# A hybrid decoder block: the first half of the second MLP matrix in quads of seven products too, all low halves on VectorE, a new order of parts

## The reference

```
h2 = rms_norm(x, norm2_g) * (1.0 + scale2) + shift2
y  = square(relu(h2 @ w_mlp1 + b_mlp1)) @ w_mlp2 + b_mlp2     # w_mlp1 1024x4096, w_mlp2 4096x1024
x  = x + gate2 * y
```

## Time and profile before

| | |
|---|---|
| median of 3 runs | 789.12 us |
| the profiled execution | 789.84 us, of which the span is 788.0 |
| TensorE busy | 777.1 us, 99% |
| weight loads (beside the matmuls) | 653.6 us, 83% |
| VectorE busy | 549.7 us, 70% |
| ScalarE busy | 339.0 us, 43% |
| GpSimd busy | 146.5 us, 19% |
| chain that ended last | TensorE 95%, VectorE 2% |

### The profile page before, as it was taken

The page is one execution under the profiler, slowest core; times in us unless marked ns, Lnnn a source line. Parts: engine busy times, 40 slices in busy tenths (PEclk is TensorE's granted clock), DMA queues, the critical chain, the costliest instruction groups (busy, mean ns, idle before and its releaser), DMA issues.

```text
span 788.0 us, 11201 instructions
## 1 busy us (share of the span) xinstructions
PE 777.1 (99%) x4216; PEld 653.6 (83%) x4216; DVE 549.7 (70%) x965; ACT 339.0 (43%) x530; POOL 146.5 (19%) x96
## 2 busy tenths in 40 slices
PE   7999999999999999999999999999999999999997
PEld 6877888788888876778889998888888888889997
DVE  6974998778988767769966899321111466688996
ACT  5475524344253276654332554432212345454331
POOL 5024344200000000000012066444454200000000
PEclk9999999999999999999999999999999999999999
DMA  9943223211221233445655245223323233213331
GB/s 351 384 136 107 80 85 103 72 62 54 74 73 54 68 119 105 145 167 176 199 187 188 81 163 212 89 98 106 104 82 106 81 106 107 80 54 107 108 108 53
DMA packets 27629, 95.29 MB, mean 121 GB/s; under 512 B 3009, under 2 KB 3393, under 8 KB 27586
## 3 DMA queue, kind: packets, MB, share of 16 engines
q1 hardware_dynamic: 27296, 94.51, 35.1%
q10 hardware_dynamic: 290, 0.20, 0.1%
HBM read 92.61 MB, written 2.10 MB: 120 GB/s over the span
## 4 chain that ended last, share of the span: by engine, by line
PE 95%; DVE 2%; ACT 1%; DMA 1%; issue 0%; SPq 0%; DVEq 0%; ACTq 0%
PE bank L1580 13%; PE bank L1582 13%; PE bank L1581 13%; PE bank L1629 5%; PE bank L1806 3%; PE bank L1808 3%; PE bank L1807 3%; PE bank L2156 3%; PE bank L2158 3%; PE bank L2157 3%; PE bank L1763 2%; PE bank L1830 2%; PE bank L1975 2%; PE bank L1765 2%; PE bank L1764 2%; PE bank L1976 2%
## 5 line engine op out<-in xcount | busy, mean ns | idle before, releaser
L442 POOL TENSOR_TENSOR w_lo<-w_raw,w_hi 128x1024 fp32r<-128x1024 f32 x49 | 125.5, 2563 | 184.8 <-ACT w_hi L503 184.8
L503 ACT ACTIVATE w_hi<-w_raw 128x1024 fp32r<-128x1024 f32 (+2 forms) x110 | 114.5, 1042 | 94.8 <-PE bank L1582 68.6
L1580 PE MATMUL bank<-h_hi,w_hi 128*128 128x512 f32 x328 | 128.1, 390 | 0.0
L1582 PE MATMUL bank<-h_hi,w_lo 128*128 128x512 f32 x328 | 127.7, 389 | 0.0
L1581 PE MATMUL bank<-h_lo,w_hi 128*128 128x512 f32 x328 | 127.6, 389 | 0.0
L1582 PEld LDWEIGHTS bank<-h_hi,w_lo 128*128 128x128 f32 x328 | 61.6, 188 | 13.0
L1581 PEld LDWEIGHTS bank<-h_lo,w_hi 128*128 128x128 f32 x328 | 61.6, 188 | 12.6
L1580 PEld LDWEIGHTS bank<-h_hi,w_hi 128*128 128x128 f32 x328 | 61.6, 188 | 12.6
L1064 DVE TENSOR_TENSOR w_lo<-w_raw,w_hi 128x1024 fp32r<-128x1024 f32 x52 | 64.1, 1239 | 9.7 <-ACT w_hi L503 9.6
L1451 DVE TENSOR_SCALAR sqr_u<-bank,col,mod 128x512 f32<-128x512 f32 x8 | 6.5, 809 | 73.9 <-PE bank L1582 73.9
L1581 PE MATMUL bank<-u_lo,w_hi 128*128 128x512 f32 x128 | 49.8, 389 | 0.0
(11 more groups left out here) (313 smaller groups left out, 1874.6 us busy)
## 6 DMA issues: line engine op xcount, KB each, us to landing
w_raw<-in_units SPq DMA_DIRECT2D x117, 512.0 KB, 3.3
ada_raw<-in_ada SPq DMA_DIRECT2D x16, 512.0 KB, 11.8
ada_even<-in_ada SPq DMA_DIRECT2D x16, 512.0 KB, 4.3
ada_odd<-in_ada SPq DMA_DIRECT2D x16, 512.0 KB, 4.2
w_raw<-in_units SPq DMA_DIRECT2D x8, 448.0 KB, 11.7
xT<-in_xt SPq DMA_DIRECT2D x4, 512.0 KB, 5.8
out<-xT SPq DMA_DIRECT2D x7, 256.0 KB, 3.9
w_raw<-in_units SPq DMA_DIRECT2D x1, 256.0 KB, 5.6
```

The costliest lines, as they stand in the source:

```text
L442: nc.gpsimd.tensor_tensor(w_lo[:, s], w_raw[:, s], w_hi[:, s].bitcast(F32), ALU.subtract).then_inc(lo_ready, 1)
L503: nc.scalar.activation(w_hi[:, s, 0:width], w_raw[:, s, 0:width], ACT.Copy).then_inc(hi_ready, 1)
L1580: mm(bank[b][:], w_hi[:, slot, j], rhs_hi(i), start=f, stop=False)
L1582: end = mm(bank[b][:], w_lo[:, slot, j], rhs_hi(i), start=False, stop=l)
```

## The change

- Units of the first half of w_mlp2 are laid out as quads (host side), and `down` is gone: `quads(0, n)` runs 16 quads. Every helper takes the half h as its first argument.
- The order on TensorE is now up 0, quads 0, up 1, quads 1. Since `h_hi` and `h_lo` are still needed for up 1, quads 0 has a ring of two homes (`RING = [2, 3]`), and the weight sums of quad n from 2 on stand in `wf_s`, one buffer outside of the homes.
- GpSimd makes no low halves from up 0 on: VectorE makes them.
- The output bias is added to `xT` by ScalarE (`out_bias`, eight instructions) with a product `GB2` that VectorE forms once.
- up 1 writes banks 4 and 5. Its first four units are split while quads 0 ends: units 0 and 1 when quad 14 is done, 2 and 3 when quad 15 is.
- In quads 1, the weight sums of the fourth quad (`sums(1, 3)`, `forms_lo(1, 3)`) stand ahead of the last token sums' low halves.
- On VectorE, `sums(h, n + 1)` follows `forms_lo(h, n)`; `parts` and `part_sums` have new places between them.
- The last two quads are done product by product in turn: products 0 to 3 of both, then 4, 5 and 6 of both. The last tile's second half of tokens may be written out after the first sums.

The core of the diff:

```diff
-        tx_home = [RL + 8 * KB + 6 * KB * i for i in range(4)] + [RA + 32 * KB, XR, XR + 6 * KB, 64 * KB]
+        tx = [tile_forms("tx", [whole(o * KB) for o in (182, 188, 194, 207, 160, 176, 213)]
+                         + [[(0, 219 * KB, 1), (1, 166 * KB, 1), (2, 200 * KB, 1)]]),
+              tile_forms("ty", [whole(o * KB) for o in (176, 182, 188, 194, 160, 207, 213, 64)])]
+        wf_s = place("wf_s", RL + 4 * KB, [P, 4, 2 * P])
...
+        RING = [2, 3]
...
+        def in_place(h, n):
+            return n == 0 or h == 1 and n >= 2
...
+        def form_slot_free(engine, h, n):
             if n == 0:
-                engine.wait_ge(group_done, G[Q0 - 2])
-            elif n <= 2:
-                engine.wait_ge(group_done, G[Q0])
+                engine.wait_ge(group_done, G[U_2[h]] - 2)
+            elif n < RING[h]:
+                engine.wait_ge(group_done, G[U_2[h]])
             else:
-                engine.wait_ge(quad_done, n - 2)
+                engine.wait_ge(quad_done, NQ * h + n - RING[h] + 1)
...
-            pool.wait_ge(lo_ready, U_1[0] + WS)
-            split_range(U_1[0] + WS, U_1[1] + WS)
...
+            def out_bias(m):
+                act.wait_ge(gb_ready, 1)
+                nc.scalar.activation(xT[:, m], xT[:, m], ACT.Identity, bias=GB2[:, m:m + 1]).then_inc(bias_ready, 1)
...
+            for h in range(2):
+                if h:
+                    split_lo(U_1[1])
+                    split_lo(U_1[1] + 1)
+                    parts(0, KC // 2 - 1)
+                    part_sums(0, KC // 2 - 1)
+                    split_lo(U_1[1] + 2)
+                    split_lo(U_1[1] + 3)
...
+                first = 4 if h else 3
+                sums(h, first)
+                for n in range(first, NQ):
+                    forms_lo(h, n)
+                    if n + 1 < NQ:
+                        sums(h, n + 1)
+                    q = (n - 3 - RING[h]) // 4
+                    if n >= 3 + RING[h] and (n - 3 - RING[h]) % 4 < 2:
+                        (parts, part_sums)[(n - 3 - RING[h]) % 4](h, q)
...
-            with pe.Fori(0, 4) as i:
-                down(i)
+            for n in range(NQ):
+                quads(0, n)
...
-            for n in range(NQ):
-                quads(n)
+            for n in range(NQ - 2):
+                quads(1, n)
+            for kinds in (range(4), (4,), (5,), (6,)):
+                for n in (NQ - 2, NQ - 1):
+                    quads(1, n, kinds)
```

More of the change, by code:

```diff
@@ L61, in hybrid_block @@
     groups = [0] * U_UQ + [4] + [1] * (N_UNITS - U_B)
+    for n in U_2:
+        groups[n:n + MH] = [0] * MH
     G = [0]
@@ L1552, in _ @@
[L1552 to L1566 removed]
+                second = gated(2 * q + 1, full, part[:, 1].rearrange("p o t -> p (o t)"))
@@ L1569, in _ @@
+            parts(1, KC // 2 - 1)
+            part_sums(1, KC // 2 - 1)
         @block.tensor
@@ L2109, in first_up, with up @@
                     end.then_inc(group_done, 1)
-            def up(half, i, j):
-                n = U_1[half] + j
+            def up(h, i, j):
+                n = U_1[h] + j
                 pe.wait_ge(lo_ready, 4 * i + (n + 1))
-                pe.wait_ge(lin_evac, 4 * i + (E_1[half] + j - 1))
-                def before(k):
-                    if k == KC // 2:
-                        pe.wait_ge(lin_evac, E_1[half])
-                product(n % WS, G[n] % 2, h_rhs(h_hi), h_rhs(h_lo), range(KC),
-                        before=before if half and j == 0 else None)
@@ L2124, in down @@
-            def down(i):
-                for j in range(4):
-                    n = U_2[0] + j
-                    pe.wait_ge(lo_ready, 4 * i + (n + 1))
-                    if j % 2 == 0:
-                        pe.wait_ge(lin_evac, 2 * i + (E_2[0] + j // 2 - 1))
-                    off = 8 * (j % 2)
-                    product(n % WS, j // 2, lambda k, o=off: u_hi[:, o + k], lambda k, o=off: u_lo[:, o + k],
-                            range(8), first=j % 2 == 0, last=j % 2 == 1,
-                            before=(lambda k, o=off: pe.wait_ge(t_lo, T_U + o + k + 1)) if j < 2 else None)
@@ L2137, in quads @@
-            def quads(n):
-                q, g = n // 4, n % 4
-                hi, lo = wf_hi[n % 3], wf_lo[n % 3]
-                b11, t1, b21, b22 = (lambda u, i, x=x: u[:, 2 * i + x // 2, HALF[x % 2]] for x in range(4))
-                t3, t2, t4 = (lambda u, i, x=x: (tx_hi if u is u_hi else tx_lo)[i][:, x] for x in range(3))
-                pe.wait_ge(lo_ready, Q0 + n + 1)
+                if h and isinstance(i, int) and j < 2:
+                    pe.wait_ge(lin_evac, E_2[0] + KC - 2)
+                else:
+                    pe.wait_ge(lin_evac, 4 * i + (E_1[h] + j - 1))
@@ new lines, in up, with quads, token_form @@
+                product(n % WS, (4 if h else 0) + j % 2, h_rhs(h_hi), h_rhs(h_lo), range(KC))
+            def quads(h, n, kinds=range(7)):
+                q, g = n // 4, n % 4
+                hi, lo = wf_hi[n % RING[h]], wf_lo[n % RING[h]]
+                u = (u_hi, u_lo)
+                def token_form(x, s, i):
+                    if x < 4:
+                        return u[s][:, 2 * i + x // 2, HALF[x % 2]]
+                    return [seg[1 + s][:, y] for seg in tx[h][i] for y in range(seg[1].shape[1])][x - 4]
+                pe.wait_ge(lo_ready, U_2[h] + n + 1)
```

424 lines of the change are left out of this document (214 added, 210 removed).

## The result

The changed kernel takes 780.50 us (median of 4 runs, 780.13 to 781.80) where the kernel before, timed beside it, takes 789.11: a ratio of 0.9894, 95% interval 0.9881 to 0.9907. The forecast was 781.7, its range 780.2 to 784.5. The profiled execution took 780.13 us, 778.3 of it the span.

A forecast was written before the change was run, and what follows sets the result against it. TensorE, busy 777.1 of 788.0 us, was taken as the bound. The terms -6.40 + 0.94 + 0.66 + 0.30 - 1.50 - 1.45 = -7.45 took the median from 789.12 to 781.7 us, range 780.2 to 784.5.

The forecast's parts named there:

- TensorE's work: Between up 0 and up 1, 672 matmuls 256 wide replace 384 that are 512 wide: 6.40 us off.
- start of up 0: At up 0's fifth unit TensorE waits for the third relu, 0.84 late plus 0.10 restart: plus 0.94 us.
- first quads 0: Waits at quads 2 and 3 of quads 0, 0.28 and 0.38 with restarts: plus 0.66 us.
- quads 7, 11, 15: In steady quads 0 these have 0.19 to spare; 0.1 loss taken for each: plus 0.3 us.
- fourth quad of quads 1: Token low halves moved behind its weight sums, so TensorE's wait there goes: minus 1.50 us.
- tail: At the kernel's end, product-by-product order leaves 0.51 us behind TensorE instead of 1.96: minus 1.45 us.
- The 2.87 stay: At the end, the last transfer after VectorE stays 2.87 us; without contention it might save 0.3.
- the forecast's own case: For the whole kernel, a time of 780.6 to 783.0 us, given 66%.
- the first (VectorE the bound): VectorE bounds quads 0; with durations 5% longer, waits at quads 7, 11, 15 and early: 784 to 785 us, 18%.
- the second (VectorE slow in up 0 for another reason): VectorE's slow rows in up 0 were not GpSimd's doing and add some 18 us: 791 us, 3%.
- The third (homes that serialise): In quads 0 two homes serialise the forms, 5.96 us a quad instead of 5.04: 793.4 us, 3%.
- The fourth (nothing lost): All new waits are zero: 779.8 us; 8% for under 780.6.

The follow-up runs named there:

- the better order: Against the changed kernel, third tile's relu ahead of first token sums' high halves; in quads 0 `sums(3)` ahead of last token low halves, `out_bias(7)` moved: 779.62 us.
- two added instructions: Changed kernel with two more 256-wide VectorE instructions on a scratch buffer behind `part_sums` in each of the first three groups of quads 0: 783.31 us.
- the old order back: Changed kernel with quads 1's last token low halves again ahead of the fourth quad's weight sums, on VectorE and ScalarE: 781.38 us.
- the old end back: Changed kernel with the last two quads one after the other again instead of product by product: 782.16 us.
- GpSimd put back, the one kernel: Changed kernel with GpSimd again making the twelve low halves of up 0 from its fifth unit on: 786.89 us, ratio 0.9971.
- the other: Changed kernel with two homes in quads 1 too, weight sums outside them in quads 0's order, last two quads still product by product: 783.64 us.
- the kernel with two homes and serial sums: Changed kernel with two homes in quads 1 (`RING = [2, 2]`), weight sums formed in the home behind the freed one: 790.70 us, ratio 1.0025.

## Why the prediction was right

| step of the prediction | forecast | measured | shown by |
|---|---|---|---|
| TensorE's work | -6.40 | -6.40 | 81.18 less the waits at quads 2 and 3 is 672 x 0.120 |
| start of up 0 | +0.94 | +0.86 | the profile; the better order takes it away |
| first quads 0 | +0.66 | +0.54 | the profile (0.29 and 0.27 by its rows); quad 3's goes with the better order |
| quads 7, 11, 15 | +0.30 | 0 | the profile; the spare by two added instructions |
| into up 1 | 0 | +0.03 | the profile |
| fourth quad of quads 1 | -1.50 | -1.51 | the old order back, for 1.16 of it |
| tail | -1.45 | -1.44 | the old end back, for 1.38 of it |
| last transfer | 0 | -0.68 | three profiles after, two before; cause open |
| sum | -7.45 | -8.60 | |

The waits and the work of TensorE came where the prediction put them and nearly in its size; the last transfer did not. Nearly all that was off was off to the same side: the -8.60 of the stages is the 8.61 between the two medians, where the forecast had 7.45.

The step that was off is "The 2.87 stay". It took the last transfer as a constant. It is 2.1 to 2.2 in three profiles of the changed kernel, and why is not shown. No row stood behind the 0.3 that the prediction named as what a transfer without a neighbour might save. This step makes more than half of the 1.2 us between 781.7 and 780.5, and without it the result would have been near 781.2, inside the forecast's own case.

For quads 7, 11 and 15 the prediction worked out 0.19 of spare and then took 0.1 of loss for each. The sum was right, and the 0.30 put on top of it was caution. The added instructions show the same 0.19.

For a stream of weight load and matmul the Trainium skill (TensorE: Matmul & The Clock Gate, Back-to-back issue gap) gives the figures by which the prediction reckoned quads 0 at 15 us slower. The trace contradicts them: 0.120 a matmul at 256 columns in quads 0 as in quads 1, against 0.227 at 512.

Of the rivals, the first (VectorE the bound) is false by 0.2 us per group; the second (VectorE slow in up 0 for another reason) fell with the squares at 0.69 and with GpSimd put back. The third (homes that serialise) is near what the kernel becomes where the sums are made in the homes, with half of the rival's price in a steady group. The fourth (nothing lost) was wrong on its waits: they are there and cost 1.4 us. Its 779.8 is only 0.7 from the result, nearer than the forecast, by luck: the transfer, which it took as fixed too, gave back half of what they cost.

## What to carry to other kernels

Where one engine sets the time, a wait can be forecast to about 0.1 us by adding up the rows of the chain behind it, as in up 0 and at quads 2, 3 and 7 here; then use the number that comes out and don't pad it. Every instruction that stands ahead in the engine's list belongs to that chain: one `part_sums` left out turned a wait of 2.0 us into a forecast of 0.3. Work taken off a slow helper engine can cost nothing on a busy one, if the helper had been slowing it. A buffer ring can be one shorter if what doesn't need the freed slot is made outside of it, but the last pair of a reordered tail asks for its slot earlier than the steady state does.

## What the runs showed of the hardware

- **The clock after a wait.** TensorE's granted clock fell to 0.50 (1.2 GHz of 2.4) just after it had taken up work behind waits of 3.45 and 1.82 us, and stood there for about 3.4 us, by the 0.66 of 465 to 470 in the one kernel and the 0.68 and 0.50 of 770 to 774 in the other; each time this cost 1.5 or 1.6 us on top of the wait. It did not fall after a wait of 3.01 us in the kernel with two homes and serial sums:

```profile
777.74 0.39 PE L2178 MATMUL bank<-u_hi,wf_hi 128*128 128x256 f32 x1 [3.01 <-DVE wf_lo L1513]
```

  What decides between the two stays open.
- **GpSimd beside VectorE.** A square of 0.69 us took 2.0 to 2.9 whenever it started while GpSimd made a low half, in ten of ten cases in two kernels, and 0.68 to 0.70 in all others. GpSimd's own 2.41 became 2.87 on the mean. Giving VectorE 12 more instructions and GpSimd none was 6 us faster.
- **The last transfer** of 128 KB ended the span 2.1 to 2.9 us after its data was ready. It was 2.9 with two others issued within 0.4 us ahead of it, but 2.1 to 2.2 and once 2.4 with the same spacing of 0.75 and 1.95, so the spacing does not explain all of it.
- **The start** up to the mark varies by 1.8 us between executions (448.79 to 450.62) in kernels that are alike there. Nearly all of it is there in the first 17 us: TensorE's wait for ScalarE's `h_hi` ends at 15.62 in the changed kernel's first profile and at 17.24 in the latest of them. What makes it is not found; the medians carry some of it.
